# Up products of a gated MLP in 512-column passes from the seventh piece on, with the halves joined by ScalarE and VectorE, and weights split three pieces ahead

## The reference

```python
def conv_gated_mlp(h, w_up, conv_w, w_down):          # h: (1, 256, 1024)
    u = h @ w_up                                      # (1024 -> 5632)
    up = jnp.pad(u, ((0, 0), (1, 1), (0, 0)))
    u = sum(up[:, t:t + S] * conv_w[t] for t in range(3))
    gate, val = jnp.split(u, 2, axis=-1)
    return (jax.nn.gelu(gate, approximate=True) * val) @ w_down
...
    h = rms_norm(x, ffn_pre_norm[l])
    x = x + rms_norm(conv_gated_mlp(h, w_up[l], ffn_conv[l], w_down[l]), ffn_post_norm[l])
```

## Time and profile before

| what | us |
|---|---|
| median of 3 runs | 1030.24 (1029.28 to 1030.42) |
| profiled execution, span from its first to its last instruction | 1027.2 |
| own time of the profiled execution | not recorded apart from the span |
| median less span (what lies around the instructions) | 3.0 |
| TensorE busy in the span | 1013.0 (99%) |
| VectorE busy | 680.7 (66%) |
| ScalarE busy | 587.5 (57%) |

### The profile page before, as it was taken

The page is one execution under the profiler, slowest core; times in us unless marked ns, Lnnn a source line. Parts: engine busy times, 40 slices in busy tenths (PEclk is TensorE's granted clock), DMA queues, the critical chain, the costliest instruction groups (busy, mean ns, idle before and its releaser), DMA issues.

```text
span 1027.2 us, 15935 instructions
## 1 busy us (share of the span) xinstructions
PE 1013.0 (99%) x6244; PEld 908.5 (88%) x6244; DVE 680.7 (66%) x932; ACT 587.5 (57%) x859; POOL 130.7 (13%) x257
## 2 busy tenths in 40 slices
PE   8999999999999999999999999999999999999997
PEld 7889999888888999999888899998888889999996
DVE  5635566655596887878865355666555869787877
ACT  5657666565446654555575666565653457455553
POOL 3353124000002000000025221230000020000000
PEclk9999999999999999999999999999999999999999
DMA  8554345444444646555454534464344645545551
GB/s 259 178 177 155 122 141 168 161 165 164 144 150 157 203 169 203 170 200 172 168 190 159 174 124 128 150 205 164 124 144 164 204 145 166 203 169 201 174 195 41
DMA packets 109037, 170.78 MB, mean 166 GB/s; under 512 B 3377, under 2 KB 72804, under 8 KB 108964
## 3 DMA queue, kind: packets, MB, share of 16 engines
q1 hardware_dynamic: 107676, 166.88, 48.8%
q10 hardware_dynamic: 1208, 2.63, 0.7%
q0 software_dynamic: 80, 0.26, 0.1%
HBM read 168.72 MB, written 1.05 MB: 165 GB/s over the span
## 4 chain that ended last, share of the span: by engine, by line
PE 95%; DVE 1%; ACT 1%; DMA 1%; issue 1%; DVEq 0%; SPq 0%; POOL 0%; POOLq 0%
PE bank L1418 28%; PE bank L1420 28%; PE bank L1419 28%; PE bank L1783 2%; PE bank L1684 1%; PE bank L1705 1%; PE bank L1776 1%; PE bank L1693 1%; PE bank L1721 1%; PE bank L1728 1%; PE bank L1773 1%; DMA w_raw<-in_w_in_dram 1%; PE bank L1735 1%; PE bank L1741 1%; DVE x_rows L1233 0%
## 5 line engine op out<-in xcount | busy, mean ns | idle before, releaser
L1053 DVE TENSOR_TENSOR w_lo<-w_raw,w_hi 128x2048 fp32r<-128x2048 f32 (+3 forms) x174 | 364.3, 2094 | 160.6 <-ACT w_hi L700 160.5
L700 ACT ACTIVATE w_hi<-w_raw 128x2048 fp32r<-128x2048 f32 (+3 forms) x174 | 304.7, 1752 | 50.3 <-PE bank L1420 48.8
L1418 PE MATMUL bank<-w_hi,hT_lo 128*128 128x512 f32 (+2 forms) x700 | 258.4, 369 | 1.5 <-DVE hT_lo L1127 0.8
L1420 PE MATMUL bank<-w_hi,hT_hi 128*128 128x512 f32 (+2 forms) x700 | 252.9, 361 | 0.0
L1419 PE MATMUL bank<-w_lo,hT_hi 128*128 128x512 f32 (+2 forms) x700 | 252.5, 361 | 0.0
L1418 PE MATMUL bank<-hT_hi,w_lo 128*128 128x256 f32 x704 | 199.4, 283 | 0.7 <-DVE hT_lo L1080 0.7
L1420 PE MATMUL bank<-hT_hi,w_hi 128*128 128x256 f32 x704 | 199.2, 283 | 0.0
L1419 PE MATMUL bank<-hT_lo,w_hi 128*128 128x256 f32 x704 | 199.2, 283 | 0.0
L1418 PEld LDWEIGHTS bank<-w_hi,hT_lo 128*128 128x128 f32 x700 | 131.5, 188 | 17.8 <-issue 3.0
L1420 PEld LDWEIGHTS bank<-w_hi,hT_hi 128*128 128x128 f32 x700 | 131.4, 188 | 14.1
L1419 PEld LDWEIGHTS bank<-w_lo,hT_hi 128*128 128x128 f32 x700 | 131.6, 188 | 13.0
(11 more groups left out here) (215 smaller groups left out, 1250.1 us busy)
## 6 DMA issues: line engine op xcount, KB each, us to landing
w_raw<-in_w_up_dram SPq DMA_DIRECT2D x44, 1024.0 KB, 4.9
w_raw<-in_w_in_dram SPq DMA_DIRECT2D x36, 1024.0 KB, 4.9
w_raw<-in_w_in_dram SPq DMA_DIRECT2D x36, 768.0 KB, 4.2
w_raw<-in_w_down_dram SPq DMA_DIRECT2D x22, 1024.0 KB, 4.8
w_raw<-in_w_out_dram SPq DMA_DIRECT2D x8, 1024.0 KB, 4.9
w_raw<-in_w_in_dram SPq DMA_DIRECT2D x8, 672.0 KB, 4.0
w_raw<-in_w_branch_mla_dram SPq DMA_DIRECT2D x4, 1024.0 KB, 4.9
w_raw<-in_w_branch_diff_dram SPq DMA_DIRECT2D x4, 1024.0 KB, 4.8
```

The source lines that it names most:

```text
L700: nc.scalar.activation(w_hi[:, n % RING, 0:nk * cols], raw[:, n % RING, 0:nk * cols], ACT.Copy).then_inc(hi_done, 1)
L1053: V.tensor_tensor(w_lo[:, n % RING, s], raw[:, n % RING, s], w_hi[:, n % RING, s].bitcast(F32), ALU.subtract).then_inc(lo_done, 1)
L1418: PE.matmul(dst, lhs[1], rhs_hi, start=start, stop=False)
L1420: return PE.matmul(dst, lhs[0], rhs_hi, start=False, stop=stop)
```

## The change

For the up pieces from c = 6 on, in each layer:

1. `hT_hi` and `hT_lo` become two halves of one tile `hT`, and the two passes that share the high weights become one pass of 512 columns (`passes_beside`): its left 256 output columns get high by high, its right ones high by low. The pass low by high stays at 256 columns and adds to the left.
2. A product now fills a whole bank, so a piece takes two banks; banks 4 to 7 are two pairs used in turn (`up_banks`). Piece c waits until the sum of piece c - 2 is done.
3. The two column halves must be added: ScalarE copies the right half into a new tile `up_low`, VectorE adds the left half to it into `up_scaled`, drains, and scales in place. Before, VectorE scaled straight from PSUM.
4. From the first down piece on, step n splits the weights of piece n + 3, not n + 2; the first down step splits both.

```diff
+BESIDE = 6
+DOWN0 = PIECES.index(("down", 0, 0, 2, 1024))
+
+def split_at(n):
+    if n < DOWN0:
+        return [n + 2]
+    return [m for m in ([n + 2, n + 3] if n == DOWN0 else [n + 3]) if m < NPIECE]
...
+        def up_banks(c):
+            pair = (c + 1) % 2
+            return high_banks[:, 2 * pair:2 * pair + 2, :]
...
@@ ScalarE
-                        if n + 2 < NPIECE and n != UP0 - 1 and (l == 0 or n):
-                            split_hi(l, n + 2)
+                        if n != UP0 - 1 and (l == 0 or n):
+                            for m in split_at(n):
+                                split_hi(l, m)
...
                         if kind == "up":
                             u, b = c // 2, c % 2
+                            if c >= BESIDE:
+                                act.wait_ge(piece_used, l * NPIECE + (RING + n + 1))
+                                nc.scalar.activation(up_low[:], up_banks(c)[:, :, SEQ:2 * SEQ], ACT.Copy).then_inc(up_low_copied, 1)
                             act.wait_ge(up_scaled_done, l * 2 * NU + (c + 1))
@@ VectorE
                 else:
+                    dve.wait_ge(up_low_copied, l * (2 * NU - BESIDE) + (c - BESIDE + 1))
+                    V.tensor_tensor(up_scaled[:, c % 2, :, :], up_banks(c)[:, :, 0:SEQ], up_low[:], ALU.add).then_inc(up_summed, 1)
+                    dve.drain()
+                    last = V.tensor_tensor(up_scaled[:, c % 2, :, :], up_scaled[:, c % 2, :, :],
                                            token_scale.rearrange("p (o q) -> p o q", o=1).broadcast_to([P, 2, SEQ]), ALU.mult)
...
                             if splits and c:
-                                split_lo(l, n + 2)
+                                for m in split_at(n):
+                                    split_lo(l, m)
@@ TensorE
+            def passes_beside(dst, w_parts, k):
+                if k == 0:
+                    PE.matmul(dst, w_parts[0], hT[:, :, k, :], start=True, stop=False)
+                last = PE.matmul(dst[:, 0:SEQ], w_parts[1], hT_hi[:, k, :], start=False, stop=False)
+                if k:
+                    last = PE.matmul(dst, w_parts[0], hT[:, :, k, :], start=False, stop=k == KD - 1)
+                return last
...
+                    if c > BESIDE + 1:
+                        pe.wait_ge(up_summed, l * (2 * NU - BESIDE) + (c - 1 - BESIDE))
```

More of the change, by code:

```diff
@@ L300, in build_trunk @@
         x = sb("x_rows", [P, NT, D])
-        hT_hi = sb("hT_hi", [P, KD, SEQ], F32R)
-        hT_lo = sb("hT_lo", [P, KD, SEQ], F32R)
+        hT = sb("hT", [P, 2, KD, SEQ], F32R)
+        hT_hi, hT_lo = hT[:, 0], hT[:, 1]
         raw = sb("w_raw", [P, RING, 2048])
@@ L370, in build_trunk @@
             up_scaled = sb("up_scaled", [P, 2, 2, SEQ], scope=four)
+            up_low = sb("up_low", [P, 2, SEQ], scope=four)
         with ExitStack() as six:
@@ L373, in build_trunk @@
             par_rows = sb("par_rows", [44, 4 * DEPTH, P], scope=six)
-        bank = [ctx.enter_context(nc.psum_tensor(f"bank{i}", [P, 512], F32)) for i in range(8)]
+        bank = [ctx.enter_context(nc.psum_tensor(f"bank{i}", [P, 512], F32)) for i in range(4)]
+        high_banks = ctx.enter_context(nc.psum_tensor("high_banks", [P, 4, 512], F32))
+        bank += [high_banks[:, i, :] for i in range(4)]
         S_BANK, O_BANK = (bank[4], bank[5]), bank[7]
@@ L415, in build_trunk @@
         root_rows_ready, scales_full, up_scaled_done = sem("root_rows_ready"), sem("scales_full"), sem("up_scaled_done")
+        up_summed = sem("up_summed")
+        up_low_copied = sem("up_low_copied")
         lat_squares, lat_normed = sem("lat_squares"), sem("lat_normed")
@@ L1104, in scale_up @@
                         last = V.tensor_tensor(up_scaled[:, c % 2, j, :], up_half(c, j), token_scale, ALU.mult)
-                else:
-                    last = V.tensor_tensor(up_scaled[:, c % 2, :, :], bank[4 + c % 4][:].rearrange("p (j q) -> p j q", j=2),
+                elif c < BESIDE:
+                    last = V.tensor_tensor(up_scaled[:, c % 2, :, :], bank[4 + c % 4][:].rearrange("p (j q) -> p j q", j=2),
+                                           token_scale.rearrange("p (o q) -> p o q", o=1).broadcast_to([P, 2, SEQ]), ALU.mult)
+                else:
+                    dve.wait_ge(up_low_copied, l * (2 * NU - BESIDE) + (c - BESIDE + 1))
+                    V.tensor_tensor(up_scaled[:, c % 2, :, :], up_banks(c)[:, :, 0:SEQ], up_low[:], ALU.add).then_inc(up_summed, 1)
+                    dve.drain()
+                    last = V.tensor_tensor(up_scaled[:, c % 2, :, :], up_scaled[:, c % 2, :, :],
                                            token_scale.rearrange("p (o q) -> p o q", o=1).broadcast_to([P, 2, SEQ]), ALU.mult)
@@ L1326, in _ @@
                         kind, c, k0, nk, cols = PIECES[n]
-                        splits = n + 2 < NPIECE and n not in (OUT0 - 1, UP0 - 1) and (l == 0 or n)
+                        splits = n not in (OUT0 - 1, UP0 - 1) and (l == 0 or n)
                         last_pair = kind == "down" and c == NU - 1 - LAG
@@ L1495, in use_piece @@
                     u, b = c // 2, c % 2
-                    if c >= 4:
+                    if 4 <= c < BESIDE:
                         pe.wait_ge(up_scaled_done, l * 2 * NU + (c - 3))
+                    if c == BESIDE:
+                        pe.wait_ge(up_scaled_done, l * 2 * NU + (c - 2))
+                    if c == BESIDE + 1:
+                        pe.wait_ge(up_scaled_done, l * 2 * NU + (c - 1))
+                    if c > BESIDE + 1:
+                        pe.wait_ge(up_summed, l * (2 * NU - BESIDE) + (c - 1 - BESIDE))
                     order = [(k, j) for k in range(8) for j in range(2)] if c == 0 else [(k, j) for j in range(2) for k in range(8)]
@@ L1505, in use_piece @@
                             turn_roots(l)
-                        last = passes(up_half(c, j), (hi[:, k, j * P:(j + 1) * P], lo[:, k, j * P:(j + 1) * P]),
-                                      hT_hi[:, k, :], hT_lo[:, k, :], k == 0, k == 7)
+                        w_parts = (hi[:, k, j * P:(j + 1) * P], lo[:, k, j * P:(j + 1) * P])
+                        if c < BESIDE:
+                            last = passes(up_half(c, j), w_parts, hT_hi[:, k, :], hT_lo[:, k, :], k == 0, k == 7)
+                        else:
+                            last = passes_beside(up_banks(c)[:, j, :], w_parts, k)
                     last.then_inc(piece_used, 1)
```

## The result

| | before | after |
|---|---|---|
| median of 4 runs each | 1029.94 us (1029.28 to 1030.42) | 1074.94 us (1069.00 to 1077.67) |
| ratio to before | | 1.0432, 95% interval 1.0413 to 1.0450 |
| span of the profiled execution | 1027.2 us | 1072.8 us |
| mean granted clock in it | 0.999 | 0.981 |

The change makes the kernel 45.0 us slower. The forecast was 1060, with a range of 1052 to 1069: the sign is right, the time is 14.9 us above the forecast and 5.9 above the range. The runs also scatter over 8.7 us, where those of before stay within 1.1.

The account below looks back on a forecast made before the run. TensorE, busy 99%, bounds the kernel, but a late `g_lo` would make it wait: 13.28 us in triples plus 1.65 per layer, 29.9 in two, on a 1027.2 span, plus 3.0, gives 1060 us; range 1052 to 1069.

Parts of the forecast that it names:

- The chain: From up piece B's first pass through split, copy, sum, scaling, `split_lo` and `g_lo` to down piece D: 7.53 us.
- Rival 4: VectorE's sum costs 1.09 us: 0.4 us more in each of 18 waits, 7 us, total 1067; chance 0.05.
- The period: One MLP triple (down piece D, up pieces A and B) takes 18.64 us, 1.66 more than 16.98; TensorE waits 1.97.
- The 3.0 added for what lies around the span: The median of the runs lies 3.0 us above the profiled span, taking 1057.1 to 1060.1.
- The bounds of the copy and the sum: Copy from PSUM 0.60 us, bound 0.69; VectorE's sum 0.76 us, bounds 0.68 and 1.09.
- TensorE's saving: Joining two 256-column passes into one of 512 saves 0.19 us per up piece, 6.1 us if nothing else changes.
- Rival 3: The 512-column pass saves nothing because its moving operand comes from two places in SBUF: 3 us, 1063; chance 0.1.
- Rival 1: The lead of `g_lo` (1.66 us) holds and TensorE saves in full: 1024 us; chance 0.05.
- The other waits: In the MLP, split weights (`w_lo`) and banks freed by the sum are ready in time, so TensorE's other new waits are covered.
- rival 2: The clock falls to 1.2 GHz in D behind each of 18 gaps, 5.47 us each: 1158 us; chance 0.05.
- The two waits before down 9: In each layer's last triple, down 9 waits 1.57 us for its `g_lo`, plus 0.08 restart: 1.65 a layer.

Follow-up runs that it names:

- run 1: Changed kernel with 16 dummy transposes (12 before down 9) on TensorE ahead of its wait for `g_lo`, filling the gaps: 1060.92 us, ratio 1.0308.
- run 5: Changed kernel with `g_lo` made first in step A, 512-column passes only for up pieces 6 to 19, last triple as before: 1024.43 us, ratio 0.9948.
- run 2: Changed kernel with VectorE making `g_lo` ahead of the sum in step A, nothing else moved: 1031.27 us, ratio 1.0017.
- run 6: Changed kernel with 8 dummy transposes (6 before down 9) on TensorE ahead of its wait for `g_lo`, half filling the gaps: 1059.68 us, ratio 1.0293.
- run 7: Kernel before the change, with three unused 128x1024 additions on VectorE ahead of `g_lo` in step A from triple 3 on: 1085.25 us, ratio 1.0543.
- run 3: Changed kernel with the weights split two pieces ahead again, as before; 512-column passes and joined halves kept: 1040.87 us, ratio 1.0110.
- run 8: Changed kernel with ScalarE's copy put ahead of its weight split in the up steps, nothing else moved: 1035.70 us, ratio 1.0058.

## Why the prediction was right, and where it failed

**The chain: right.** Worked out 7.53 us from B's first pass to D, measured 7.58. By terms (measured, then predicted): ScalarE's start 0.26 and 0.27, split 1.82 and 1.82, copy with its handover 0.68 and 0.64, sum 0.79 and 0.76, scaling 0.61 and 0.61, `split_lo` 2.20 and 2.20, `g_lo` with TensorE's start 1.22 and 1.23. So prices read from other lines of before held for instructions that before does not have. ScalarE's start is 0.26 by the prediction's own rows too (436.79 less 436.53). Rival 4, a dear sum, falls.

**The period: right.** 18.64 predicted, 18.73 measured; TensorE's gap 1.97 and 1.99. With the gaps filled the kernel takes 1060.9 against the 1060 of the forecast, and that it comes so near is partly luck. The span of run 1 is 1058.9 us, 1.8 above the 1057.1 that was worked out. The 3.0 added for what lies around the span was too much: it set a median against the span of another execution, and by execution it is 1.8 (1074.62 less 1072.8 in after, 1060.73 less 1058.9 in run 1). The bounds of the copy and the sum were not needed.

**TensorE's saving: right.** 0.19 us a wide piece, 0.184 in run 5. Rival 3, that the 512-column pass saves nothing, falls. In after A takes 5.59 us (387.54 to 393.13) where it took 5.75, so 0.16 is saved there; what B saves goes into the wait, as the prediction said. Rival 1, that the lead holds, is false in the changed kernel and true in run 5, where the order that forbade it is changed.

**The other waits: right.** TensorE waits nowhere in the MLP for `w_lo` or for the banks that the sum frees.

**The clock: wrong.** The failed step is rival 2, "The clock falls in the new gaps". It was set aside at 0.05, on rows near the start where TensorE was busy for half the time and the clock read 1.00, so that "the granted clock should stay at 1.00" and the sum has nothing for it. Those rows show pauses at another place and of another make-up; they did not show a still stand of 2 us behind a long busy stretch, and no row of before does. In its place the profile of after shows 11 stretches at the half level behind 16 gaps, 17.4 us; the waits came to 28.0, where 29.9 was forecast. Runs 1, 2, 6 and 7 show what it hangs on. Gaps of 1.8 to 2.6 us can bring the half level, though not each of them does; gaps of up to 0.9 did not, nor did four of 1.4 (two each in runs 3 and 8). It doesn't need the 512-column up passes (run 7 has none), and they don't bring it about by themselves (run 1 has them all).

The rival's price was wrong too. It was 5.47 us, a whole D at half speed behind each of 18 gaps, 98 in all. In the profile it is 1.58 us behind 11 of 16, 17.4 in all. The two errors go together: a fall of the clock was thought of as all or nothing, so a case between 1060 and 1158 was not in the list.

On such a loss the Trainium skill, TensorE: Matmul & The Clock Gate, section HAM oscillation, says that waits between bursts of matmuls can throttle the engine again each time, and prices this at half the time spent at the lower level. The waits of its case are longer than these and each is paid for; here five of 16 were not. The stretches here last about 3.4 us each; by that page 11 of them cost an estimated 18.7 us. The measured 17.4 agrees in size.

**The two waits before down 9: right in runs 1 and 6, absent in after.** In run 1 D's end and down 9 lie 1.55 us apart (518.84 to 520.39), where 1.57 was worked out without the restart. In after the D of the last triple runs slowly in both layers, and its delay of 1.58 covers the wait of 1.65. The list has 16 waits, not 18.

**Left open.** Why the first five gaps of layer 0 in after, alike in length to the others, left the clock at 1.00. The stretch isn't tied to the end of the wait either. In after it begins between 0.2 and 1.5 us behind D's first pass (the last one at about 1049.26, below), in run 7 up to 1.4 us behind it or, four times, up to 0.3 us ahead of it.

```profile
1047.80 0.47 PE L1452 MATMUL bank<-w_hi,g_lo 128*128 128x512 f32 x1 [1.82 <-DVE g_lo L1149]
...
1049.26 0.62 PE L1452 MATMUL bank<-w_hi,g_lo 128*128 128x512 f32 x1
```

The times of after vary by 8.7 us from run to run, and their mean clocks go with them (0.988 at 1069.0, 0.979 at 1077.7); this would fit another number of stretches in each run, but only one run of after has a trace here.

## What to carry to other kernels

Where one engine bounds the kernel, find what it waits for next, read the lead of that instruction (1.66 us here) and count every instruction that an edit puts ahead of it on any in-order engine. Put the awaited instruction first: the same parts in another order go from 4.3% slower to 0.2% slower (run 2), and with the last triple left as it was to 0.5% faster (run 5). And price a new gap of TensorE twice, for the wait and for the clock behind it, each time with part of the work behind it and not all or nothing.

## What was not expected of the hardware

- A single gap of 2.56 us, behind an unbroken busy stretch, was followed by a stretch at the 1.2 GHz level that began 1.2 us after the work had gone on (run 2). Gaps of 1.8 us were followed by one in 11 of 16 cases, those of run 6 (up to 0.9 us) and four of 1.4 us (runs 3 and 8) never. In run 7 four of the ten stretches began inside the gap.
- Sixteen idle transposes in each gap (twelve before down 9), 1.91 us of TensorE's time that give nothing, saved 14.0 us in all (run 1); half as many did as well (run 6).
